# A two-block model kernel: modulation pieces moved between stages, small DVE and ACT reorderings, and softmax steps written with separate reduces

## What is computed

```python
def first_block(x, ...):
    h = _swiglu(_rms_norm(x, ffn1_pre_norm), ffn1_w_in, ffn1_w_out)
    x = x + 0.5 * _rms_norm(h, ffn1_post_norm)
    m = _token_mixing(_rms_norm(x, mix_pre_norm), ...)   # retention + neighbourhood attention, gated
    x = x + _rms_norm(m, mix_post_norm)
    h = _swiglu(_rms_norm(x, ffn2_pre_norm), ffn2_w_in, ffn2_w_out)
    return x + 0.5 * _rms_norm(h, ffn2_post_norm)

def second_block(x, c, ...):
    mod = einsum('bd,lde->lbe', silu(c), ada_w) + ada_b      # (2 layers, 6 * 1024)
    for i in range(2):
        shift1, scale1, gate1, shift2, scale2, gate2 = split(mod[i], 6)
        y = (moba_attention, diff_attention)[i](x * (1 + scale1) + shift1, ...)
        x = layer_norm(ALPHA * x + (1 + gate1) * y, ln_g[i, 0], ln_b[i, 0])
        y = square(relu((x * (1 + scale2) + shift2) @ w_up)) @ w_down
        x = layer_norm(ALPHA * x + (1 + gate2) * y, ln_g[i, 1], ln_b[i, 1])
    return x
# diff_attention, per head: w = softmax(q1 k1^T) - lam * softmax(q2 k2^T); o = rms_norm(w @ v) * g * (1 - lam_init)
```

## Time and profile before

| | |
|---|---|
| median of 3 runs | 1293.27 us (1291.62 to 1295.24) |
| the profiled execution | 1293.27 us |
| its span, first to last instruction | 1291.5 us |
| mean granted clock of PE | 0.980 |
| busy: PE, DVE, ACT, POOL | 96%, 72%, 47%, 7% |
| DMA | 274.31 MB, mean 212 GB/s |

### The profile page before, as it was taken

How to read it: one execution, slowest core, us unless ns; L and a number is a source line. 1 busy time by engine, 2 the same in 40 slices (tenths; PEclk the granted TensorE clock), 3 DMA queues, 4 the chain that set the end, 5 groups by cost and what they waited for, 6 DMA issues and landing times.

```text
span 1291.5 us, 14651 instructions
## 1 busy us (share of the span) xinstructions
PE 1233.6 (96%) x5777; PEld 1012.3 (78%) x5777; DVE 932.0 (72%) x1349; ACT 609.4 (47%) x801; POOL 93.4 (7%) x136
## 2 busy tenths in 40 slices
PE   7999999999999999999999989999989986999996
PEld 6888877887888878888788768888867764888885
DVE  6789867866556698888775458886878776755546
ACT  7344445535664454434555535443435653625340
POOL 2100220003400010000000000000000000000000
PEclk9999999999999999999999979999999997999999
DMA  9999885545445598997473336787835531366530
GB/s 303 330 334 324 309 259 192 173 142 173 159 151 175 179 334 320 309 311 256 141 246 130 131 130 244 252 302 278 292 115 192 183 127 69 137 210 224 181 145 33
DMA packets 132916, 274.31 MB, mean 212 GB/s; under 512 B 6240, under 2 KB 51504, under 8 KB 132848
## 3 DMA queue, kind: packets, MB, share of 16 engines
q1 hardware_dynamic: 114992, 209.80, 47.4%
q0 software_dynamic: 17792, 63.56, 14.5%
q10 hardware_dynamic: 64, 0.02, 0.0%
HBM read 270.41 MB, written 2.93 MB: 212 GB/s over the span
## 4 chain that ended last, share of the span: by engine, by line
PE 87%; DVE 7%; ACT 2%; issue 2%; DMA 2%; ACTq 0%; DVEq 0%
PE ps L448 26%; PE ps L450 26%; PE ps L449 26%; PE ps L558 3%; DVE lo_w L1262 1%; PE ps L522 1%; DMA w_raw<-in_w_mix_in 1%; PE ps L825 1%; PE ps L698 1%; ACT hi_w L912 1%; PE ps L685 1%; DVE piece_acc L1441 1%; PE ps L722 1%; PE ps L810 0%; PE ps L808 0%
## 5 line engine op out<-in xcount | busy, mean ns | idle before, releaser
L1262 DVE TENSOR_TENSOR lo_w<-w_raw,hi_w 128x2048 fp32r<-128x2048 f32 x197 | 447.4, 2290 | 99.7 <-ACT hi_w L912 99.4
L448 PE MATMUL ps<-hi_w,xT_hi 128*128 128x512 f32 x1120 | 449.4, 401 | 9.9 <-DVE xT_lo L1283 5.4
L450 PE MATMUL ps<-lo_w,xT_hi 128*128 128x512 f32 x1120 | 439.7, 393 | 0.0
L449 PE MATMUL ps<-hi_w,xT_lo 128*128 128x512 f32 x1120 | 439.1, 392 | 0.0
L912 ACT ACTIVATE hi_w<-w_raw 128x2048 fp32r<-128x2048 f32 x197 | 373.2, 1916 | 45.7 <-DMA w_raw<-in_w_mix_out 11.8
L448 PEld LDWEIGHTS ps<-hi_w,xT_hi 128*128 128x128 f32 x1120 | 212.4, 190 | 56.8 <-issue 12.8
L450 PEld LDWEIGHTS ps<-lo_w,xT_hi 128*128 128x128 f32 x1120 | 212.2, 189 | 45.9
L449 PEld LDWEIGHTS ps<-hi_w,xT_lo 128*128 128x128 f32 x1120 | 212.8, 190 | 41.9
L448 PE MATMUL ps<-hi_w,hT_hi 128*128 128x512 f32 x464 | 183.4, 395 | 5.7 <-DVE hT_lo L1425 5.7
L449 PE MATMUL ps<-hi_w,hT_lo 128*128 128x512 f32 x464 | 181.8, 392 | 0.0
L450 PE MATMUL ps<-lo_w,hT_hi 128*128 128x512 f32 x464 | 181.6, 391 | 0.0
(11 more groups left out here) (221 smaller groups left out, 887.1 us busy)
## 6 DMA issues: line engine op xcount, KB each, us to landing
w_raw<-in_ffn_w_in SPq DMA_DIRECT2D x86, 512.0 KB
aux<-in_ada_w POOLq DMA_DIRECT2D x34, 1024.0 KB, 6.5
w_raw<-in_mlp_w_up SPq DMA_DIRECT2D x32, 1024.0 KB
w_raw<-in_mlp_w_down SPq DMA_DIRECT2D x32, 1024.0 KB
w_raw<-in_w_mix_in SPq DMA_DIRECT2D x26, 1024.0 KB
w_raw<-in_ffn_w_out SPq DMA_DIRECT2D x22, 1024.0 KB
area<-in_ada_w POOLq DMA_DIRECT2D x14, 1024.0 KB, 7.5
w_raw<-in_moba_w_in SPq DMA_DIRECT2D x12, 1024.0 KB
```

Of the source, the lines that this page charges most:

```text
L448: pe.matmul(dst, lhs_hi, rhs_hi, start=start, stop=False)
L449: pe.matmul(dst, lhs_lo, rhs_hi, start=False, stop=False)
L450: return pe.matmul(dst, lhs_hi, rhs_lo, start=False, stop=stop)
L1262: vec.tensor_tensor(lo_w[:, ring_slot(u), :], w_raw[:, ring_slot(u), :], hi_w[:, ring_slot(u), :].bitcast(F32), ALU.subtract).then_inc(w_l ...
```

## The change

It is a bundle. What the parts do:

- `PIECES` goes from 8, 9, 7 to 9, 9, 6, and FFN1 starts its pieces with block 0. POOL issues piece 0 before the constants, where it had waited for `w_lo` to reach 7 behind them, and the post-norm row before piece 1 and not after piece 3.
- The fold, one fused transpose and reduce, becomes a transpose into the second half of `piece_acc`, a wait and a reduce. The next piece's first step no longer waits for `piece_done`.
- `small_vectors` runs behind block 1 of FFN1, on ACT and DVE.
- At the start, unit 1 is split after the fourth quarter of x, on both engines.
- At the end of a SwiGLU ACT splits the unit `next_unit + 1` before the last `hidden_hi`.
- The scores are no longer negated. Neighbourhood attention: a reduce with max, and a tiny multiplication by -1. MOBA and DIFF: one pass over both parts of a head (768 columns), two reduces, one multiplication by -1, in the place of the four fused instructions.
- `combine` divides both parts by their totals (two scalings more) and the norm takes the plain epsilon, so `head_eps` goes.

```diff
-PIECES = (8, 9, 7)
+PIECES = (9, 9, 6)
...
-                    if i == 3 and between is not None:
+                    if i == 1 and between is not None:
                         between()
                 next_unit = u0 + 3 * N_FF
                 split_hi(next_unit - 1)
                 hidden_hi(b0 + N_FF - 2, N_FF - 2)
                 activation(b0 + N_FF - 1, N_FF - 1)
                 split_hi(next_unit)
+                split_hi(next_unit + 1)
                 hidden_hi(b0 + N_FF - 1, N_FF - 1)
-                split_hi(next_unit + 1)
...
-            split_hi(1)
             quarter_out(0, 1, 1, f1)
-            for u in range(2, AHEAD):
+            for u in range(1, AHEAD):
                 split_hi(u)
...
-                                             ACT.Exp, scale=-1.0, bias=top[:, 0, t:t + 1],
-                                             accum_out=total[:, h % 2, t:t + 1])
+                                             ACT.Exp, bias=top[:, 0, t:t + 1], accum_out=total[:, h % 2, t:t + 1])
...
-                        if p >= 1:
-                            vec.wait_ge(piece_done, p)
...
+                then(vec.transpose(piece_acc[:, 1, :], piece_acc[:, 0, :]))
                 vec.tensor_reduce(piece_sums[:, 16 * p:16 * p + 16],
-                                  piece_acc[:, 0, :].rearrange("p (b i) -> p b i", i=32), AX.X, ALU.add,
-                                  apply_transpose=True).then_inc(piece_done, 1)
+                                  piece_acc[:, 1, :].rearrange("p (b i) -> p b i", i=32), AX.X, ALU.add)\
+                   .then_inc(piece_done, 1)
...
-                    piece = p0 + i - first if 0 <= i - first < n_pieces else None
+                    piece = p0 + i if i < n_pieces else None
...
-            split_lo(1)
             quarter_split(0, 1, 1)
-            for u in range(2, AHEAD):
+            for u in range(1, AHEAD):
                 split_lo(u)
...
-                    vec.tensor_reduce(top[:, 0, :], na_scores.rearrange("p (t n) -> p t n", t=NT), AX.X, ALU.min)\
-                       .then_inc(at_m, 1)
+                    then(vec.tensor_reduce(top[:, 1, :], na_scores.rearrange("p (t n) -> p t n", t=NT), AX.X, ALU.max))
+                    vec.tensor_scalar(top[:, 0, :], top[:, 1, :], -1.0, None, ALU.mult).then_inc(at_m, 1)
...
-                    for e in range(2):
-                        for t, cols in enumerate([slice(0, P), slice(P, 3 * P)]):
-                            ins = vec.tensor_tensor_reduce(
-                                out=probs[:, e * 3 * P:(e + 1) * 3 * P][:, cols], in0=bank(e)[:, cols],
-                                in1=causal[:, cols], scale=-HD ** -0.5, scalar=3.0e38, op0=ALU.add, op1=ALU.min,
-                                accum_out=top[:, e, t:t + 1])
-                    ins.then_inc(at_m, 1)
+                    src = bank(0, 2).rearrange("p (e n) -> p e n", e=2)[:, :, 0:3 * P]
+                    dst = probs.rearrange("p (e n) -> p e n", e=2)
+                    mask = causal[:, :].unsqueeze(1).broadcast_to([P, 2, 3 * P])
+                    then(vec.scalar_tensor_tensor(out=dst, in0=src, scalar=HD ** -0.5, in1=mask, op0=ALU.mult,
+                                                  op1=ALU.add))
+                    vec.tensor_reduce(top[:, :, 0], dst[:, :, 0:P], AX.X, ALU.max)
+                    then(vec.tensor_reduce(top[:, :, 1], dst[:, :, P:3 * P], AX.X, ALU.max))
+                    vec.tensor_scalar(top[:, :, :], top[:, :, :], -1.0, None, ALU.mult).then_inc(at_m, 1)
...
-                    vec.scalar_tensor_tensor(out=head_eps[:, c % 4, :], in0=first, scalar=P * SUBLN_EPS, in1=first,
-                                             op0=ALU.mult, op1=ALU.mult)
-                    then(vec.reciprocal(inv[:, 0:NT], second))
-                    then(vec.scalar_tensor_tensor(out=inv[:, NT:2 * NT], in0=first, scalar=lam[:, 0:1], in1=inv[:, 0:NT],
-                                                  op0=ALU.mult, op1=ALU.mult))
+                    then(vec.reciprocal(inv[:, :], total[:, c % 2, :]))
+                    then(vec.tensor_scalar(inv[:, 2:4], inv[:, 2:4], lam[:, 0:1], None, ALU.mult))
+                    for t in range(NT):
+                        ins = vec.tensor_scalar(probs_w[:, tiles[t]], probs[:, tiles[t]], inv[:, t:t + 1], None, ALU.mult)
+                    then(ins)
...
-                    then(vec.tensor_tensor(squares, squares, head_eps[:, k:k + n, :], ALU.add))
...
             pool.wait_ge(w_lo, AHEAD)
+            modulation(0, 1, aux)
...
-            pool.wait_ge(w_lo, RING + 1)
-            modulation(0, 4, aux)
             row(row_ffn, d["ffn1_post_norm"])
-            modulation(4, PIECES[0] - 4, aux)
+            modulation(1, PIECES[0] - 1, aux)
```

More of the change, by code:

```diff
@@ L191, in two_blocks_kernel @@
         head_rstd = sb("head_rstd", [P, 4 * NT])
-        head_eps = sb("head_eps", [P, 4, NT])
         shift = sb("shift", [P, NT])
@@ L1192, in exps @@
                             pr = probs[:, e * 3 * P:e * 3 * P + P] if t == 0 else probs[:, e * 3 * P + P:(e + 1) * 3 * P]
-                            ins = act.activation(pr, pr, ACT.Exp, scale=-1.0, bias=top[:, e, t:t + 1],
+                            ins = act.activation(pr, pr, ACT.Exp, bias=top[:, e, t:t + 1],
                                                  accum_out=total[:, c % 2, 2 * e + t:2 * e + t + 1])
@@ L1459, in mod_columns, with swiglu @@
                 then(ins)
-            def swiglu(u0, b0, first, p0, n_pieces, between=None, sums=None):
+            def swiglu(u0, b0, p0, n_pieces, between=None, sums=None):
                 def product(b, i):
@@ L1616, in _ @@
             vec.wait_ge(c_done, 1)
-            swiglu(U_FFN1, B_FFN1, 1, 0, PIECES[0], small_vectors)
+            swiglu(U_FFN1, B_FFN1, 0, PIECES[0], small_vectors)
             after_rms(S_FFN1, U_MIX, row_ffn, 0.5)
@@ L1628, in _ @@
                         vec.wait_ge(at_e, h)
-                    then(vec.scalar_tensor_tensor(out=na_scores, in0=bank(h % 2), scalar=-NA_D ** -0.5,
+                    then(vec.scalar_tensor_tensor(out=na_scores, in0=bank(h % 2), scalar=NA_D ** -0.5,
                                                   in1=bias[h % 2].rearrange("p t n -> p (t n)"),
-                                                  op0=ALU.mult, op1=ALU.subtract))
-                    vec.tensor_reduce(top[:, 0, :], na_scores.rearrange("p (t n) -> p t n", t=NT), AX.X, ALU.min)\
-                       .then_inc(at_m, 1)
+                                                  op0=ALU.mult, op1=ALU.add))
+                    then(vec.tensor_reduce(top[:, 1, :], na_scores.rearrange("p (t n) -> p t n", t=NT), AX.X, ALU.max))
+                    vec.tensor_scalar(top[:, 0, :], top[:, 1, :], -1.0, None, ALU.mult).then_inc(at_m, 1)
                 if slot == 4:
@@ L1734, in _ @@
             after_rms(S_MIX, U_FFN2, row_a, 1.0)
-            swiglu(U_FFN2, B_FFN2, 0, PIECES[0], PIECES[1], sums=first_modulation)
+            swiglu(U_FFN2, B_FFN2, PIECES[0], PIECES[1], sums=first_modulation)
             after_rms(S_FFN2, U_MOBA, row_ffn, 0.5)
@@ L1781, in combine @@
                     vec.wait_ge(at_t, ab + c)
-                    first, second = total[:, c % 2, 0:NT], total[:, c % 2, NT:2 * NT]
-                    vec.scalar_tensor_tensor(out=head_eps[:, c % 4, :], in0=first, scalar=P * SUBLN_EPS, in1=first,
-                                             op0=ALU.mult, op1=ALU.mult)
-                    then(vec.reciprocal(inv[:, 0:NT], second))
-                    then(vec.scalar_tensor_tensor(out=inv[:, NT:2 * NT], in0=first, scalar=lam[:, 0:1], in1=inv[:, 0:NT],
-                                                  op0=ALU.mult, op1=ALU.mult))
-                    for t, cols in enumerate([slice(0, P), slice(P, 3 * P)]):
-                        ins = vec.scalar_tensor_tensor(out=probs_w[:, cols], in0=probs[:, 3 * P:6 * P][:, cols],
-                                                       scalar=inv[:, NT + t:NT + t + 1], in1=probs[:, cols],
-                                                       op0=ALU.mult, op1=ALU.add)
+                    then(vec.reciprocal(inv[:, :], total[:, c % 2, :]))
+                    then(vec.tensor_scalar(inv[:, 2:4], inv[:, 2:4], lam[:, 0:1], None, ALU.mult))
+                    tiles = [slice(0, P), slice(P, 3 * P)]
+                    for t in range(NT):
+                        ins = vec.tensor_scalar(probs_w[:, tiles[t]], probs[:, tiles[t]], inv[:, t:t + 1], None, ALU.mult)
+                    then(ins)
+                    for t in range(NT):
+                        second = probs[:, 3 * P:6 * P][:, tiles[t]]
+                        ins = vec.scalar_tensor_tensor(out=probs_w[:, tiles[t]], in0=second, scalar=inv[:, 2 + t:3 + t],
+                                                       in1=probs_w[:, tiles[t]], op0=ALU.mult, op1=ALU.add)
                     ins.then_inc(at_w, 1)
@@ L1796, in norms @@
                     k = c % 4
```

(5 more changed lines are left out.)

## The result

The changed kernel takes 1304.17 us (median of four runs, 1302.49 to 1306.45), the kernel before 1293.74 beside it; the ratio is 1.0088, with a 95% interval of 1.0075 to 1.0100. It is slower by 0.9%, where 1296.3 was forecast and 1300.6 was the end of the range. All 32 executions of the changed kernel on record, these four included, took 1302.49 to 1308.51, with a median of 1304.98. The profiled execution took 1305.24 us with a span of 1303.4: 11.9 more span than before.

What follows compares the result with a forecast made beforehand. PE was taken to bound the kernel, so only its waits and clock count. The terms 0.3 + 0.6 + 0 - 4.2 + 1.0 + 4.6 + 0.7 = +3.0 gave 1296.3 us; range 1290.5 to 1300.6.

Steps and rivals of the forecast that it cites:

- What bounds the kernel: Whole kernel: PE is busy for 1233.6 of 1291.5 us, so only its waits and clock count.
- MLP1: End of the first MLP: without its last piece, PE's 3.33 us wait and the half clock go; -4.2 us.
- DIFF: Differential attention: dearer scores and combine lengthen the DVE and ACT period from 7.14 to 8.2 us; +4.6 us.
- The half-clock stretch added to it: Differential attention: more standing of PE can cost one more stretch at half clock, 1.4 us, half likely; +0.7 us.
- MOBA: Tail of the MOBA attention: the last head's scores take 1.03 us longer and delay its exponentials; +1.0 us.
- the one on FFN1's blocks: FFN1's blocks 0 to 2: first halves of pieces start on DVE at 31.4, 46.5 and 67.0 us.
- The 0.6 of the forecast: FFN1's block 2: `small_vectors` two blocks earlier, behind a fuller block, makes `hidden_lo` late for PE; +0.6 us.
- ACT's swap: FFN1's end: PE waits 1.65 us more, taken up by its existing 2.50 us wait before 199.88; 0 us.
- The start: Second weight unit: its split, moved behind x's fourth quarter, ends at 19.4 where PE wants it at 19.11; +0.3 us.
- late piece 0: FFN1's start: piece 0's first half lands at 34 us, delaying blocks 0 and 2; 1300.6 us in all, chance 0.14.

Runs made afterwards that it cites:

- `hidden_lo` first: The changed kernel with both halves of pieces 0, 1 and 2 behind the block's `hidden_lo`; 1304.28 us, ratio 1.0078 to the kernel before.
- piece 1 held back: The changed kernel with the load of piece 1 held until the low part of unit 7 is made; 1305.93 us, ratio 1.0092 to the kernel before.

## Why the prediction was wrong, point by point

**What bounds the kernel**: right, and the steps behind FFN1 came out nearly as summed. MLP1 gave -4.7 for -4.2, with `hidden_lo` 0.25 us before PE's need and no half clock. DIFF +4.8 for +4.6, with its period, its first wait before the third weights (+0.8 for +0.7) and the heads' transpose (+2.1 for +2.1) where they were put. The half-clock stretch added to it (+0.7) did not come: the stretches in DIFF are as long after as before. MOBA's +2.3 for +1.0 is a term mis-sized: I counted one head, and the ring of ACT's split and DVE's put a second one into the same chain (1.8 in all); the other 0.5 is half clock. That FFN1 apart the sum came out within 0.3 (2.4 for 2.1) is in part luck, since MOBA's 1.3 too much stands against MLP1's 0.5 and the 0.7 that did not come.

**The step that failed** is the one on FFN1's blocks: "block 0's first half starts at 31.4, block 1's at 46.5, and block 2's, behind 5.4 of `small_vectors`, at 67.0". Block 0's was right (31.79). Block 1's came at 54.27 and not at 46.5, for ahead of it in DVE's queue stood the split of weight unit 8, whose landing came at 50.1; I had taken the landings of weights as given. I had asked what the DMA engines do to piece 0 and not what piece 0 and piece 1 do to the weights. Once block 1 is put where it was, the prediction's own arithmetic gives the rest: `hidden_lo` at 57.02, a block of 15.1 without idle and 5.4 of `small_vectors` make 77.5; it started at 77.47. So block 2's wait is the same error again, with `small_vectors` as its second condition (the run with it back). The 0.6 of the forecast had no room for this: by its own count DVE was full from block 0 to block 2, so what block 1 comes late is carried to block 2 in full. FFN1's blocks 1 and 2 cost 6.8 (4.7 + 2.1) where 0.6 stood.

**The cover spent twice.** That ACT's swap costs nothing, being taken up by the wait before 199.88, was right: in the run with the swap put back that wait returned. But it holds 4.2 us with its clock, and the swap itself takes more of it than the 1.65 that I wrote: 2.3 by waiting and 2.8 by the clock in the changed kernel. With all but the pieces changed, start and swap use it up and FFN1 ends level. With the pieces too, 2.1 + 4.7 + 2.1 + 5.1 come in front of it, and 14.0 less 4.2 is 9.8. So by the profiles the pieces alone cost FFN1 1.5 and the rest alone 0.2, and together 9.8: the parts of this bundle don't add up, and I had summed them.

**The start**: +2.1 for +0.3; the size hangs on when the clock rises, which differs between profiles of kernels with the same start.

**The rival "late piece 0"** came true only where the pieces were moved alone. The changed kernel is slower than its 1300.6 by another mechanism.

**Open**: shortening block 1's wait (`hidden_lo` first, piece 1 held back) gave no time back, so what the late unit costs at the end of the kernel is read from the account and not shown by a run. How a queue's share hangs on packet size was read from counts and bytes in several traces, but the run that was to change the size did not change it; and in the 4 us before the stretch shown the counts are 320 and 463, so they need not be near-equal everywhere. What the split fold and the start cost by themselves is below what the runs resolve.

## What to carry to other kernels

When a load is moved earlier, ask which other loads it meets, and read their landing times, not only its own. Here two queues moved as many packets each, so the one with the larger packets got most of the bytes. A wait downstream hides only as much as it is long, its half clock included; when several edits of a bundle rely on it, subtract it once from their sum. And look for the engine's idle time inside the stage before moving work to another one: the gain was to be had 5 us away from where it was lost.

## What the runs showed of the hardware

With both queues at work, 314 packets of 4 KB and 308 of 1 KB went out in the same 4 us, at 380 GB/s in all; with POOL's queue empty, SP's alone moved 1158 packets in those 4 us. Halving the rows of POOL's loads from 2 KB to 1 KB hardly made its packets smaller (3.6 KB on average, not 3.9). Waits of PE of 1.83, 1.89 and 2.79 us each had a stretch at half clock behind them, while one of 3.36 us (block 2, with piece 1 held back) had none: the length of a single wait did not tell whether the clock falls.
